# A hybrid decoder layer on one core: attention, output projection and feed-forward put into one phase, with the dense work of four finished blocks laid between the steps of the next four

## The reference, cut to what matters

```python
h = rms_norm(x, norm_pre_mix[l]); proj = h @ w_in[l]                  # 2048 tokens, width 1024
q, k, v, qi, ki, wi, hq, hf, hi, hg = split_columns(proj)             # rope on q, k, qi, ki
att_out = dsa_attention(q, k, v, qi, ki, wi)                          # 8 heads of 64
hg_out  = hgrn2_mixer(hq, hf, hi, hg, ...)
mix = concatenate([att_out, hg_out]) @ w_out[l]                       # 1024 -> 1024
x = x + rms_norm(mix, norm_post_mix[l])
h2 = rms_norm(x, norm_pre_ffn[l])
ff = (silu(h2 @ w_gate[l]) * (h2 @ w_up[l])) @ w_down[l]              # 1024 -> 2816 -> 1024
x = x + rms_norm(ff, norm_post_ffn[l])

# dsa_attention, for each block of 128 queries:
rel = relu(einsum('bthd,bsd->btsh', qib, ki)); iscore = sum over heads of rel * wib, causal
idx = top_k(iscore, 256)                 # each query keeps its 256 best causal keys
p = softmax(q . k[idx] * HEAD_DIM ** -0.5); o = p @ v[idx]
```

## Time and profile before

| | |
|---|---|
| median of 3 runs | 3766.92 us (3763.57 to 3768.46) |
| the profiled execution | 3761.64 us, span 3759.7 us |
| PE busy (share of the span) | 3408.5 us (91%) |
| PEld busy | 2946.7 us (78%) |
| DVE busy | 2052.4 us (55%) |
| ACT busy | 1490.8 us (40%) |
| mean granted TensorE clock | 0.936 |

### The profile page before, as it was taken

How to read it: one execution, slowest core, us unless ns; L and a number is a source line. 1 busy time by engine, 2 the same in 40 slices (tenths; PEclk the granted TensorE clock), 3 DMA queues, 4 the chain that set the end, 5 groups by cost and what they waited for, 6 DMA issues and landing times. The chain is left out here.

```text
span 3759.7 us, 44974 instructions
## 1 busy us (share of the span) xinstructions
PE 3408.5 (91%) x17984; PEld 2946.7 (78%) x17984; DVE 2052.4 (55%) x2889; ACT 1490.8 (40%) x2022; POOL 212.0 (6%) x416
## 2 busy tenths in 40 slices
PE   8999999989678888788887997999999999999998
PEld 8999998888556666677677885888788878888887
DVE  3467677777477888888883333332333233324332
ACT  3344454444355656656654333222222232222221
POOL 0000010010211120010000110000000000000000
PEclk9999999999656889989988998999999999999999
DMA  4434333322100000000002443233323232333232
GB/s 169 151 121 141 129 125 126 112 101 73 49 21 21 18 14 11 18 11 11 5 3 94 157 153 123 101 119 112 117 101 120 104 124 99 120 107 123 94 119 90
DMA packets 83558, 338.80 MB, mean 90 GB/s; under 512 B 7328, under 2 KB 28448, under 8 KB 64928
## 3 DMA queue, kind: packets, MB, share of 16 engines
q1 hardware_dynamic: 76448, 315.06, 23.8%
q10 hardware_dynamic: 6912, 20.97, 1.4%
HBM read 274.60 MB, written 61.41 MB: 89 GB/s over the span
## 5 line engine op out<-in xcount | busy, mean ns | idle before, releaser
L1848 PE MATMUL ps_dense<-h_hi,wd_hi 128*128 128x512 f32 x1408 | 551.9, 392 | 33.3 <-DVE h_lo L1798 19.3
L1792 DVE TENSOR_TENSOR wd_lo<-wd_raw,wd_hi 128x2048 fp32r<-128x2048 f32 (+1 forms) x136 | 303.2, 2230 | 499.9 <-ACT wd_hi L1747 499.9
L1849 PE MATMUL ps_dense<-h_lo,wd_hi 128*128 128x512 f32 x1408 | 550.5, 391 | 0.0
L1850 PE MATMUL ps_dense<-h_hi,wd_lo 128*128 128x512 f32 x1408 | 550.5, 391 | 0.0
L657 PE MATMUL PJ<-w_hi,h_hi 128*128 128x342 f32 (+1 forms) x1280 | 418.0, 327 | 4.2 <-DVE w_lo L490 4.2
L1747 ACT ACTIVATE wd_hi<-wd_raw 128x2048 fp32r<-128x2048 f32 (+1 forms) x136 | 252.5, 1856 | 405.8 <-PE ps_dense L1870 234.4
L659 PE MATMUL PJ<-w_hi,h_lo 128*128 128x342 f32 (+1 forms) x1280 | 410.8, 321 | 0.0
L658 PE MATMUL PJ<-w_lo,h_hi 128*128 128x342 f32 (+1 forms) x1280 | 410.7, 321 | 0.0
L1313 PEld LDWEIGHTS SC<-V,pT 128*128 128x128 f32 x2176 | 312.9, 223 | 79.2 <-ACT pT L1051 79.2
L1313 PE MATMUL SC<-V,pT 128*128 128x64 f32 x2176 | 335.3, 310 | 42.7 <-ACT pT L1051 42.7
L1848 PEld LDWEIGHTS ps_dense<-h_hi,wd_hi 128*128 128x128 f32 x1408 | 266.2, 189 | 91.3 <-DVE h_lo L1798 19.7
(11 more groups left out here) (205 smaller groups left out, 6037.6 us busy)
## 6 DMA issues: line engine op xcount, KB each, us to landing
wd_raw<-in_w_gu SPq DMA_DIRECT2D x88, 1024.0 KB, 4.8
wd_raw<-in_w_down SPq DMA_DIRECT2D x40, 1024.0 KB, 4.8
w_raw<-in_w_in SPq DMA_DIRECT2D x20, 1368.0 KB, 6.3
w_raw<-in_w_in SPq DMA_DIRECT2D x20, 1352.0 KB, 6.1
row_h<-proj_d SPq DMA_DIRECT2D x16, 1024.0 KB, 8.2
proj_d<-stage SPq DMA_DIRECT2D x40, 342.0 KB, 5.3
proj_d<-stage SPq DMA_DIRECT2D x40, 338.0 KB, 3.7
row<-proj_d SPq DMA_DIRECT2D x16, 676.0 KB, 4.0
```

Of the source, the lines that this page charges most:

```text
L1792: nc.vector.tensor_tensor(w_lo[:, k % 2, w], w_raw[:, w], w_hi[:, k % 2, w].bitcast(F32), ALU.subtract).then_inc(w_lo_ready, 1)
L1848: nc.tensor.matmul(o, w_hi[:, f % 2, w], h_hi[:, c, :], start=(c == 0), stop=False)
L1849: nc.tensor.matmul(o, w_hi[:, f % 2, w], h_lo[:, c, :], start=False, stop=False)
L1850: last = nc.tensor.matmul(o, w_lo[:, f % 2, w], h_hi[:, c, :], start=False, stop=(c == KD - 1))
```

## The change

The phases `attention_phase`, `out_phase` and `ffn_phase` become one `mixer_phase`. The dense work (output projection and feed-forward) of a superblock of four blocks is cut into a list of `items`: 4 `turn` (transposes of the mixed rows), 16 `out` pieces (128 tokens x 512 columns, half of the 1024 inputs), 5 `gap` (normalisation and transposes), 44 `up` pieces (8 x 3 matmuls of 512 columns) and 48 `down` pieces (at most 4 x 3 matmuls). The items of superblock `s` (s = 0, 1, 2) are spread, by a table of weights, over the slots between the steps of blocks `4s + 4` to `4s + 7`: slots `i` inside the index scores, `s` after the first scores, `A` before the transposes of a head, `B` and `C` before its products with `V`. Each engine runs its share of an item (`after(n)`, PE `item(n)`) at the same slot. The items of superblock 3 follow the last block (`TAIL`).

To make room: PSUM gives 4 banks to `SA` (now also for the turned probabilities and all dense transposes), 1 to `SC`, 3 to the dense pieces (`PJ_d`). The down product no longer stays in PSUM over all 22 hidden tiles: it is summed over groups of 4 tiles, and each group is added by DVE into `acc` in SBUF (the first group is copied by ACT); the output projection likewise in 2 groups. Weights stand in a ring of 4 units of 512 KB, where the raw tile and its `_lo` tile share one place. `silu` is built from `Tanh`. `hid` holds 5 hidden tiles. `h2_d` is gone. The loops over superblocks are written out.

```diff
+GROUPS = [(f, min(f + 4, NF)) for f in range(0, NF, 4)]
+HID = 5
+RING = 4
+def mixer_phase(nc, a, proj_d, mix_d, x1_d, out):
+    items = []
+    for s in range(NS):
+        items += [("turn", s, i) for i in range(TS)]
+        items += [("out", s, kg, n, i) for kg in range(2) for n in range(2) for i in range(TS)]
+        items += [("gap", s, k) for k in range(5)]
+        made = 0
+        for g, (f0, f1) in enumerate(GROUPS):
+            last = f1 - 1 if g >= NG - 2 else f1
+            items += [("up", s, f, m) for f in range(made, last + 1) for m in range(2)]
+            made = last + 1
+            items += [("down", s, g, n, i) for n in range(2) for i in range(TS)]
+    cost = {"turn": 0.35, "out": 1.0, "gap": 0.9, "up": 2.0, "down": 1.0}
...
+    for u in range(RING, len(units)):
+        freed = unit_last[u - RING]
+        loads_after.setdefault(freed, []).append(u)
+        lag = 1 if items[freed][0] == "up" else 2 + (u % 2)
+        split_at = max(freed, split_at, min(freed + lag, unit_first[u] - 1))
+        splits_after.setdefault(split_at, []).append(u)
...
+        h_hi = sb("h2_hi", [P, KD, SB], F32R)
+        h_lo = sb("h2_lo", [P, KD, SB], F32R)
+        w_hi = sb("wd_hi", [P, RING, D], F32R)
+        w_lo, w_raw = sb_two("wd_lo", [P, RING, D], "wd_raw", [P, RING, D])
+        hid, tile = sb_two("hid", [P, HID, 2, SB], "tile", [P, HID, D])
+        acc = sb("acc", [P, TS, D])
         SA = psum("SA", [P, 2, 1024])
-        SBk = psum("SBk", [P, 2, 512])
         SC = psum("SC", [P, 512])
+        PJ = psum("PJ_d", [P, 3, 512])
...
+            def load_unit(u):
+                kind, s = units[u][0:2]
+                if u >= RING:
+                    wait_piece(sp, items[unit_last[u - RING]])
...
+            def split_unit(u):
+                act.wait_ge(w_in[u % RING], 16 * (u // RING + 1))
+                s_.activation(w_hi[:, u % RING, :], w_raw[:, u % RING, :], ACT.Copy).then_inc(w_hi_ready, 1)
...
+                if x[0] in ("out", "down") and x[2] > 0:
+                    half, i = x[3:]
+                    wait_piece(dve, x)
+                    wait_piece_read(dve, (x[0], s, x[2] - 1, half, i))
+                    to = acc[:, i, half * 512:(half + 1) * 512]
+                    v.tensor_tensor(to, to, PJ[:, piece[x] % 3, :], ALU.add).then_inc(pj_dve, 1)
...
+            for b in range(NB):
+                if 2 <= b + 1 < NB:
+                    wait_pair_read(pe, use["keys", b + 1])
+                    pe.wait_ge(doubled["qi"], b)
+                    for c in range(pairs_of(b + 1)):
+                        for h in range(IH):
+                            idx(b + 1, c, h)
+                            if h % 4 == 3:
+                                fill(("i", b, c, h // 4))
+                wait_pair_read(pe, use["keys", b])
+                pe.wait_ge(doubled["q"], b + 1)
+                scores(b, 0)
+                fill(("s", b))
+                for h in range(HEADS):
+                    if h + 1 < HEADS:
+                        scores(b, h + 1)
+                    elif b + 1 < NB:
+                        for key in openings(b + 1):
+                            open_split(key)
+                    fill(("A", b, h))
+                    for p in range(pairs_of(b)):
+                        turn_probs(b, h, p)
+                        fill(("BC"[p], b, h))
+                        values(b, h, p)
+            for n in range(*TAIL):
+                item(n)
```

More of the change, by code:

```diff
@@ new lines, in mixer_phase, with read_by @@
+    at = {x: n for n, x in enumerate(items)}
+    cost = {"turn": 0.35, "out": 1.0, "gap": 0.9, "up": 2.0, "down": 1.0}
+    piece, pieces = {}, []
+    for x in items:
+        if x[0] in ("out", "up", "down"):
+            piece[x] = len(pieces)
+            pieces.append(x)
+    def read_by(x):
+        return "act" if (x[0] == "out" and x[2] == 0) or (x[0] == "down" and x[2] == 0) else "dve"
+    read_count = {}
+    for x in pieces:
+        read_count[x] = 1 + sum(1 for y in pieces[:piece[x]] if read_by(y) == read_by(x))
@@ new lines, in mixer_phase, with units_of @@
+    units, unit_first, unit_last = [], [], []
+    def units_of(x):
+        if x[0] == "up":
+            return [x]
+        if x[0] == "out":
+            return [("out", x[1], x[2], x[3], j) for j in range(2)]
+        f0, f1 = GROUPS[x[2]]
+        return [("down", x[1], x[2], x[3], j) for j in range((f1 - f0) // 2)]
+    unit_no = {}
+    for n, x in enumerate(items):
+        if x in piece:
+            for u in units_of(x):
+                if u not in unit_no:
+                    unit_no[u] = len(units)
+                    units.append(u)
+                    unit_first.append(n)
+                    unit_last.append(n)
+                unit_last[unit_no[u]] = n
@@ new lines, in mixer_phase, with first_slot @@
+    fills, done = {}, 0
+    for s in range(NS - 1):
+        def first_slot(b):
+            return slots.index(("s", b))
+        window = slots[first_slot(TS * (s + 1)):(first_slot(TS * (s + 2)) if s + 2 < NS else len(slots))]
+        mine = [n for n, x in enumerate(items) if x[1] == s]
+        total_w, total_c = sum(weight[k] for k in window), sum(cost[items[n][0]] for n in mine)
+        so_far, spent = 0.0, 0.0
+        for k in window:
+            so_far += weight[k]
+            first = done
+            while done <= mine[-1] and spent + cost[items[done][0]] <= total_c * so_far / total_w + 1e-6:
+                spent += cost[items[done][0]]
+                done += 1
+            fills[k] = (first, done)
+        assert done == mine[-1] + 1
@@ L1053, in _, with fill @@
+            def fill(key):
+                for n in range(*fills.get(key, (0, 0))):
+                    after(n)
             for key in openings(0):
@@ L1250, in _, with take @@
             t = nc.tensor
+            taken = []
             pe.wait_ge(const_in, 3 * 16)
-            def turn(src, to, n):
-                for j in range(n):
-                    last = t.transpose(to[:, j * P:(j + 1) * P], src(j), ident[:])
-                return last
+            def take(key):
+                assert use[key] == len(taken), key
+                taken.append(key)
+                wait_pair_free(pe, key)
             def open_split(key):
```

1159 lines of the change are left out of this document (542 added, 617 removed).

## The result

The changed kernel takes 3920.43 us (median of 4 runs, 3918.91 to 3921.79), the kernel before 3765.24 us beside it: ratio 1.042, 95% interval 1.039 to 1.045. It is 155 us slower where 3585 us, 4.8% less, was forecast. The profiled execution has a span of 3917.1 us.

The account below looks back on a forecast made before the run. VectorE was taken to bound the attention half and TensorE the dense half, with TensorE bounding all once mixed. Terms: 967.0 + 175.3 + 8 + 1978 + 451 = 3579 us of span, stated as 3585; range 3475 to 3705.

Parts of the forecast that it names:

- TensorE's work in the mixed windows: Blocks 4 to 15: attention at 3.82 us a key block and the like, 617.5, plus dense 1228.2, makes 1845.7 us.
- the rival built on it: Attention half fuller: if 83% weight-load share is full, attention needs 752 us, not 617.5; total 3720, chance 0.09.
- DVE is busy near 76%: Sign of a right forecast: VectorE's busy share from block 5 on, beside a clock of 0.97 or more.
- PE is then the bound of every window, and at a clock near 1: Mixed windows: TensorE needs 546, 621, 679 us, VectorE 70 to 77% of that, ScalarE under 55%; pieces fill TensorE's pauses.
- Waits that stay or are new: Mixed windows: 9 us a block, 108 over twelve, plus 24 for blocks 4, 8 and 12; 132 us in all.
- (a): Block ends: third set of turned rows waits for the PSUM pair VectorE frees last; 42.3 us in 10 waits.
- the three engines hold each other up: Attention slots join TensorE, ScalarE and VectorE in fixed order; one more microsecond at each of 96 heads, 3681, chance 0.17.
- Weights ... I cost it at nothing; without cover each microsecond of delay counts 48 times: Ring of down weights: loading, copying and subtracting two units takes 9.4 us within 10.9 of pieces; cost nothing.
- The slower rival: Ring of weights: late loads or splits; 3.8 us at each of 48 halves, 182 us, ends the gain; slower 0.04.
- the sign that was named for it: Waits on weight splits in the tail, where only the pieces cover them; named as showing the forecast wrong, no size.
- The tail: Superblock 3 after block 15: 409.4 of TensorE work, plus start 10, norm 14, end 14, clock 4; 451 us.
- Openings of a superblock: Blocks 4, 8 and 12 hold turned rows, normalisation and GpSimd's roots: 8 us more each, 24.

Follow-up runs that it names:

- e5: The change with the shorter lag of e1, and each item's weight splits run at the start of the next item on ScalarE and VectorE: 3762.91 us, ratio 1.001.
- e8: On top of e1, ScalarE rounds only 64 of 1024 columns of each weight unit behind the first ring: 3743.64 us, ratio 0.995.
- e12: e5's deferred splits together with e8's narrow rounding on ScalarE: 3749.8 us, ratio 0.996.
- e1: The change, with a weight unit freed by a group's last down piece split one item later instead of two or three: 3831.24 us, ratio 1.016.
- e9: On top of e5, the gap item with the first turned tile of the normed rows priced at 5.0 in the placement instead of 0.9: 3748.73 us, ratio 0.9955.
- e10: On top of e5, the four turned tiles at a superblock's start priced at 2.0 each in the placement instead of 0.35: 3761.32 us, ratio 0.9993.
- e11: On top of e5, the placement prices of e9 and e10 together: 3770.8 us, ratio 1.0025.
- e14: On top of e5, squares of the second norm's rows moved from the last output items to the first two gap items, each placed at 3.0: 3748.1 us, ratio 0.996.
- e4: The change with nothing interleaved: all dense pieces of the four superblocks run after block 15, attention order kept: 4365.94 us, ratio 1.159.

## Why the prediction was wrong

*TensorE's work in the mixed windows*: right. 1845.7 us forecast, 1852.8 found, so the 3.82 us for each key block holds. For block 14 the forecast had 200 us of work and "about 210" in all; in the change it lasts 223.1 us for a price of 199.6, and in e5 202.9 for 199.8:

```profile
2923.40:3126.30 202.90, 198.65 (x1056) 168.02 (x1055) 135.70 (x198) 87.45 (x112) 2.31 (x1) 1.00 0.18 62
```

Weight loads are busy 168.02 / 202.90 = 83% at a clock of 1.00 with next to no waits: the 83% of the earlier trace rows, now in a mix with attention, so in this kernel 83% did mean full. The Trainium skill, "Perfetto Trace Analysis", section "Identifying the Most-Contended Engine", takes the busy share of weight loads as the measure of how near TensorE is to full, and the trace agrees. But the rival built on it divided loads that the low clock had lengthened: of the 622.3 us of loads, 178 lie in spells at the lower clock, where a load takes 0.33 us instead of 0.19. At full clock they would be some 547 us, and 547 / 0.828 = 661 (an estimate), not 752. By the rival the attention of this block needs (58.1 + 14.7) x 752 / 617.5 = 89 us instead of 73, and the block 216; it lasted 202.9.

*"DVE is busy near 76%"*: wrong, 57 to 60%. The 70 to 77% were shares of PE's work and not of the windows; over the forecast's own 1978 us the 1345 us of VectorE's work are 68%. VectorE did 1310, and the windows grew. *"PE is then the bound of every window, and at a clock near 1"*: wrong as it stood. No engine was the bound. The clock was 0.93.

*"Waits that stay or are new"*, 132 us: **the step that failed.** It measured 390, of which 104 at the low clock, for which the term had nothing: 178 in blocks 4, 8 and 12, where 51 were forecast, and some 212 in the other nine, where 81 were. The part carried over from the old trace, (a), was too large (27.4 us in 10 waits, 42.3 forecast). The part for the new order was far too small. I took the waits that the old order had, and added a few microseconds a block for the new one. What I left out is that ScalarE and VectorE also run in order, and that a piece puts its own share on them (tanh, copy, up to three splits of 1.05 and 1.23 us, squares that wait for a root) ahead of the exponential, the copy `pT` and the score pass that TensorE's next step needs. I had that as a rival ("the three engines hold each other up", 3681, 0.17), with the right mechanism and one microsecond a head; it was mis-sized too. e5, e8 and e12 show it for the splits: 68 to 88 us. For the rest (tanh and sums ahead of an attention step) it is argued from the timeline, and wasn't tried. Over all, e1 and e5 take 97 us out of the windows, of 265 that they lie over the forecast; what made the greater part of the miss is located below, but no run takes it away.

*"Weights ... I cost it at nothing; without cover each microsecond of delay counts 48 times"*: wrong. The check of lengths was sound (9.4 us of loads and splits in 10.9), but I reckoned with when a split could run and not with when the plan runs it. 62.9 us of waits, and 89 us with what follows (e1). The slower rival had the right place, the ring, and the sign that was named for it, waits on weight splits in the tail, came. But it had loads that start late and a part of the search in front of a split, where the runs show a split that the plan puts late: e1 leaves the loads as they are, and these waits go. It is also too small for that rival's numbers, 89 us where it needed 182 or more.

*The tail*, 451: 524.7, of which the same late splits are 53; the remaining 471 are within 20 us of the sum. The start and the norm together wait 26 us (forecast 10 + 14), right.

*Openings of a superblock*, 8 us more in each of blocks 4, 8 and 12: mis-sized. In e9, with all mended that I could mend, stalls and low clock in these three blocks are 42, 71 and 56 us, 169 where (9 + 8) x 3 = 51 were forecast; the other nine have some 111 for 81. Placement (e9, e10, e11, e14) moved these waits about and took 14 us off the whole, hardly any of it in these three blocks. By the timelines a chain through ScalarE, GpSimd and VectorE stands there, each of which must pass in order. No run shortens that chain, so the cause of these 118 us stays open.

*The whole*: 3920 - 89 (late splits) - 68 (splits in front) - 14 (norm placed later) = 3749. The span of e9, 3751.0, lies 172 us over the forecast's 3579: 153 in the windows, 118 of them in three blocks, and 20 in the tail, less 2 in blocks 0 to 3. The range, 3475 to 3705, doesn't reach even that. And by e4 the chance of slower was far too small: what the new order and the piece form cost without any overlap, 601 us with the late splits and some 390 without, was the first thing to price, and I never priced it; for the piece form the forecast had 451 against 428.7, 22 us a superblock, and for the order of attention nothing of its own. Two slips in the recorded sums changed nothing: the last attention window of the earlier trace rows ends 3 us behind the last reciprocal, so 902.7 is 900 by the rule of the other boundaries, and 3466 on the median's scale is 3473, not 3471.

## What to carry to other kernels

When work of another kind is slotted between the steps of a chain, price not only the bound engine's queue but every engine's: list for one slot what stands in program order ahead of the step that the bound engine waits for next. The shares that nobody waits for soon go behind that step; the same edit costs time if a ring has no room for the delay, so count what slack a deferral uses up. And price the new form without any overlap first: the gain of interleaving is measured from there, not from the kernel before.

## What the hardware showed

A wait can cost more than its length. In the timeline of the tail, behind a wait of 3.65 us, TensorE's products start 0.43 us apart instead of 0.226, at 1.2 GHz. The clock record of the trace has 42 spells at the lower level, 480 us in all, in the kernel before, and 81 spells, 597 us, in the change; with both orders mended (e5) they are 58 and 499. In e4, with the same price of work, the excess at the low clock behind block 3 is some 311 us, where it was 96 before. The Trainium skill, "TensorE: Matmul & The Clock Gate", section "Part 1: The HAM clock gate", says that the lower rate is the engine's resting state and that activity lifts it. The trace agrees: with no further wait, the same products of the tail start 0.23 us apart again. I had allowed 4 us for the clock in the tail and nothing in the windows, and it was 28 and 104.
